# A causal depthwise convolution split over engines: a fourth 128-channel tile leaves TensorE for ScalarE products and GpSimd sums

## What is computed

```python
x = x + 0.5 * _swiglu_ffn(_rmsnorm(x, ffn_norm[i, 0]), ...)
h = _rmsnorm(x, mix_norm[i])
# mixer of layer 0
ab = h @ w_in + b_in;  a, b = split(ab);  u = a * sigmoid(b)
u = depthwise_causal_conv(u, dw) + dw_b        # 31 taps for each of 1024 channels
u = silu(layernorm(u, ln_g, ln_b))             # over the 1024 channels
m = u @ w_out + b_out
# mixer of layer 1: causal differential attention, 8 heads
x = x + m
x = x + 0.5 * _swiglu_ffn(_rmsnorm(x, ffn_norm[i, 1]), ...)
```

## Time and profile before

| | us |
|---|---|
| median of 3 runs | 974.65 (973.72 to 975.8) |
| profiled execution, its own time | 976.0 |
| its span in the trace | 974.2 |
| TensorE busy | 965.4 (99%) |
| VectorE busy | 768.0 (79%) |
| ScalarE busy | 480.6 (49%) |
| GpSimd busy | 56.4 (6%) |

### The profile page before, as it was taken

The page is one execution under the profiler, slowest core; times in us unless marked ns, Lnnn a source line. Parts: engine busy times, 40 slices in busy tenths (PEclk is TensorE's granted clock), DMA queues, the critical chain, the costliest instruction groups (busy, mean ns, idle before and its releaser), DMA issues.

```text
span 974.2 us, 12520 instructions
## 1 busy us (share of the span) xinstructions
PE 965.4 (99%) x4539; PEld 798.4 (82%) x4539; DVE 768.0 (79%) x1445; ACT 480.6 (49%) x751; POOL 56.4 (6%) x75
## 2 busy tenths in 40 slices
PE   8999999999999999999999999999999999999998
PEld 6788888888988888888888888888778788888887
DVE  6758787877967988888788878787768889888872
ACT  6635353465235444444544535354777764444431
POOL 0200000010200200000000000000333100000000
PEclk9999999999999999999999999999999999999999
DMA  8974545562853754545455463635423455454521
GB/s 288 344 310 161 227 155 232 203 235 103 254 178 135 238 215 174 210 178 204 185 195 216 150 238 147 241 142 203 173 87 130 174 180 197 185 205 183 198 104 43
DMA packets 29660, 185.62 MB, mean 191 GB/s; under 512 B 3504, under 2 KB 3632, under 8 KB 9392
## 3 DMA queue, kind: packets, MB, share of 16 engines
q1 hardware_dynamic: 25056, 169.88, 45.8%
q0 software_dynamic: 4416, 15.09, 4.9%
q10 hardware_dynamic: 144, 0.07, 0.0%
HBM read 183.98 MB, written 1.05 MB: 190 GB/s over the span
## 4 chain that ended last, share of the span: by engine, by line
PE 95%; DMA 2%; DVE 1%; ACT 1%; issue 0%; POOL 0%; ACTq 0%
PE pg L470 17%; PE pg L474 16%; PE pg L476 16%; PE acc L470 13%; PE acc L476 13%; PE acc L474 13%; PE acc L661 3%; PE pt L559 1%; PE acc L771 1%; DVE w_lo L1263 1%; DMA raw<-in_units 1%; DMA diags<-in_conv_diags 1%; PE pt L790 1%; ACT w_hi L867 0%; PE pt L752 0%; DMA first<-in_first 0%
## 5 line engine op out<-in xcount | busy, mean ns | idle before, releaser
L1263 DVE TENSOR_TENSOR w_lo<-raw,w_hi 128x1024 fp32r<-128x1024 f32 x316 | 370.4, 1222 | 17.2 <-ACT w_hi L867 16.0
L867 ACT CAST w_hi<-raw 128x1024 fp32r<-128x1024 f32 x316 | 313.2, 1047 | 14.6 <-DMA raw<-in_units 14.4
L470 PE MATMUL pg<-w_hi,a_hi 128*128 128x512 f32 x720 | 283.1, 393 | 0.0
L476 PE MATMUL pg<-w_hi,a_lo 128*128 128x512 f32 x720 | 280.7, 390 | 0.0
L474 PE MATMUL pg<-w_lo,a_hi 128*128 128x512 f32 x720 | 280.6, 390 | 0.0
L1385 DVE STREAM_TRANSPOSE mix<-hs 32x128 f32<-32x128 f32 x592 | 179.2, 303 | 8.9
L470 PEld LDWEIGHTS pg<-w_hi,a_hi 128*128 128x128 f32 x720 | 135.3, 188 | 29.3 <-issue 1.4
L476 PEld LDWEIGHTS pg<-w_hi,a_lo 128*128 128x128 f32 x720 | 135.3, 188 | 28.1
L474 PEld LDWEIGHTS pg<-w_lo,a_hi 128*128 128x128 f32 x720 | 135.3, 188 | 26.9
L1377 DVE SCALAR_TENSOR_TENSOR hs<-pg,rstd,hs 128x256 f32<-128x256 f32 x80 | 38.4, 484 | 103.4 <-ACT hs L912 103.4
L912 ACT ACTIVATE hs<-pg,rstd 128x256 f32<-128x256 f32 x80 | 37.9, 475 | 162.5 <-PE pg L476 162.5
(11 more groups left out here) (147 smaller groups left out, 661.7 us busy)
## 6 DMA issues: line engine op xcount, KB each, us to landing
raw<-in_units SPq DMA_DIRECT2D x158, 1024.0 KB, 5.3
diags<-in_conv_diags POOLq DMA_DIRECT2D x20, 512.0 KB, 4.8
raw<-in_units SPq DMA_DIRECT2D x8, 256.0 KB, 6.2
gain<-in_ffn_norm POOLq DMA_DIRECT2D x3, 512.0 KB, 5.2
xs<-in_x SPq DMA_DIRECT2D x4, 256.0 KB, 5.9
gain<-in_mix_norm POOLq DMA_DIRECT2D x2, 512.0 KB, 6.2
xg<-in_conv_b_in POOLq DMA_DIRECT2D x2, 512.0 KB, 4.3
out_y<-xs SPq DMA_DIRECT2D x4, 256.0 KB, 2.0
```

What stands on the lines that cost most here:

```text
L470: mm = pe.matmul(dst[j], stat_hi, m_hi, start=first, stop=False)
L476: mm = pe.matmul(dst[j], stat_lo, m_hi, start=False, stop=last)
L867: nc.scalar.copy(w_hi[n % RING][:, cols], raw[n % RAW][:, cols]).then_inc(hi_done, 1)
L1263: nc.vector.tensor_tensor(w_lo[n % RING][:, cols], raw[n % RAW][:, cols], w_hi[n % RING][:, cols].bitcast(F32), ALU.subtract).then_inc(lo_ ...
```

## The change

Tile 3 (128 channels) leaves TensorE. ScalarE multiplies its shifted rows by the weights, 31 products of 128x256. GpSimd adds them, two products (128x512) at a time, and lastly adds the two halves. So VK is 4, DVE_TILES is 3, GROUPS falls from 10 to 8 and the diagonal halves from 20 to 16. The products lie in the memory of the sigmoid (`pair_sum`) and in one half of the gain buffer. VectorE's sums lie in PSUM from its 16th tap on. Its order changes: more taps before `glu(3)`, tile 2 lags by 7, the addition of `b_out` moves behind the `rest` calls, and two `tick`s are cut into halves that stand elsewhere. SyncE issues diagonal loads 4 to 15, behind its load of unit u+12. TensorE's order of turns changes.

```diff
-VK = 3
+VK = 4
+DVE_TILES = 3
+PAIRS = -(-W // 2)
-EARLY = 4
-TAPS_DONE = [VK * W - EARLY - 2, VK * W - EARLY - 1, VK * W]
+AT_CHUNK = [4, 9, 15]
+LATE = 7
+TAPS_DONE = [DVE_TILES * W - LATE - 2, DVE_TILES * W - LATE - 1, DVE_TILES * W]
+        pair_sum = sil.rearrange("p t n -> p (t n)")
+        def pair_at(p):
+            return gain[:, 1, p % 2 * 2 * T:(p % 2 + 1) * 2 * T] if p else pair_sum
# SyncE
+            def load_diags(h):
+                sp.wait_ge(diag_used, h - DIAG_RING + 1)
+                sp.dma_start(diags[:, h % DIAG_RING, :], conv_diags[h]).then_inc(diag_loaded_again[h % DIAG_RING], 16)
             for n in range(PIECED, UNITS):
                 load(n)
+                if n == UNIT0[CONV] + 12:
+                    for h in range(DIAG_RING, HALVES):
+                        load_diags(h)
# GpSimd
+            def sum_pair(p):
+                n = min(2, W - 2 * p) * T
+                pool.wait_ge(product_done, min(2 * p + 2, W))
+                if p > 1:
+                    pool.wait_ge(pair_summed, p - 1)
+                nc.gpsimd.tensor_tensor(pair_sum[:, 0:n], pair_sum[:, 0:n], pair_at(p)[:, 0:n], ALU.add).then_inc(pair_summed, 1)
                 if kind == "turn" and a == CONV:
-                    for h in range(DIAG_RING, HALVES):
-                        load_diags(h)
+                    for p in range(1, PAIRS):
+                        sum_pair(p)
+                    pool.wait_ge(pair_summed, PAIRS - 1)
+                    nc.gpsimd.tensor_tensor(cv[:, DVE_TILES, :], pair_sum[:, 0:T], pair_sum[:, T:2 * T], ALU.add) \
+                        .then_inc(pair_summed, 1)
+                    pool.wait_ge(pair_summed, PAIRS)
+                    load_gain(a + 2)
# TensorE, order of the turns
-                for g in range(2, 6):
-                    taps(g)
+                taps(2)
+                taps(3)
                 pe.wait_ge(u_placed, KT)
+                taps(4)
+                taps(5)
+                for g in range(3):
+                    turn_group(g)
+                turn_group(3).then_inc(c_turned, 1)
                 taps(6)
-                for g in (2, 3):
-                    turn_group(g)
-                taps(7)
-                turn_group(4)
-                turn_group(5).then_inc(c_turned, 1)
-                taps(8)
-                turn_group(6)
                 turn_tile(0)
                 turn_tile(1).then_inc(c_turned, 1)
-                turn_group(0)
-                turn_group(1)
-                turn_tile(2).then_inc(c_turned, 1)
-                taps(9)
-                turn_group(7)
-                turn_group(8)
-                turn_group(9).then_inc(c_turned, 1)
+                taps(7)
+                turn_tile(2)
+                turn_tile(3).then_inc(c_turned, 1)
+                for g in range(4, 7):
+                    turn_group(g)
+                turn_group(7).then_inc(c_turned, 1)
# ScalarE
+                def products(p0, p1):
+                    if p0 == 0:
+                        act.wait_ge(chunk_out, 2 * (c0 + chunks))
+                    for p in range(p0, p1):
+                        if p >= 3:
+                            act.wait_ge(pair_summed, p - 2)
+                        for j in range(2 * p, min(2 * p + 2, W)):
...
+                            mm.then_inc(product_done, 1)
                 sigmoids(chunks - 1)
+                products(0, 3)
                 take(0)
+                products(3, 4)
                 take(1)
                 place(chunks - 1)
+                products(4, 6)
                 for g in range(2, GROUPS):
                     take(g)
-                    if g in (4, 6):
-                        round_half(u + 2 * chunks + AHEAD, (g - 4) // 2)
+                    products(min(3 * g, PAIRS), min(3 * g + 3, PAIRS))
+                    if g in (5, 6):
+                        round_half(u + 2 * chunks + AHEAD, g - 5)
# VectorE
+                def dve_sum(k, j):
+                    if AT_CHUNK[2] - (LATE if k == 2 else 0) <= j < W - 1:
+                        return pg[:, k // 2, k % 2 * T:(k % 2 + 1) * T]
+                    return cv[:, k, :]
+                def both(j0, j1):
+                    for j in range(j0, j1):
+                        tap(0, j)
+                        tap(1, j)
+                        if j >= LATE:
+                            tap(2, j - LATE)
                 glu(0)
-                dve.wait_ge(b_out_loaded, 16)
-                for t in range(TT):
-                    mm = nc.vector.tensor_tensor(xs[:, t, :], xs[:, t, :], b_out, ALU.add)
-                link(mm)
                 tick(u + 2)
                 tick(u + 3)
+                both(0, AT_CHUNK[0])
                 glu(1)
+                both(AT_CHUNK[0], AT_CHUNK[0] + 3)
                 tick(u + 4)
+                both(AT_CHUNK[0] + 3, AT_CHUNK[1])
                 glu(2)
+                both(AT_CHUNK[1], AT_CHUNK[2])
                 tick(u + 5)
                 glu(3)
+                both(AT_CHUNK[2], W)
+                for j in range(W - LATE, W):
                     tap(2, j)
+                    if j in (W - 5, W - 3):
+                        rest_half(u + 6 + AHEAD, (j - W + 5) // 2)
                 for n, j in enumerate((2, 0, 1, 3)):
                     dve.wait_ge(c_turned, n + 1)
                     mm = stats(j)
-                    if n == 0:
-                        tick(u + 6)
-                    if n == 2:
-                        tick(u + 7)
                 for kt in range(2, KT):
                     rest(kt)
+                    if kt < 4:
+                        rest_half(u + 7 + AHEAD, kt % 2)
+                dve.wait_ge(b_out_loaded, 16)
+                for t in range(TT):
+                    mm = nc.vector.tensor_tensor(xs[:, t, :], xs[:, t, :], b_out, ALU.add)
+                link(mm)
                 for w in range(3):
                     tick(u + 2 * chunks + w)
```

More of the change, by code:

```diff
@@ L270, in trunk @@
         diag_loaded = [sem(f"diag_loaded{i}") for i in range(DIAG_RING)]
+        diag_loaded_again = [sem(f"diag_loaded_again{i}") for i in range(DIAG_RING)]
         diag_used = sem("diag_used")
@@ L279, in trunk @@
         tap_done = sem("tap_done")
+        product_done = sem("product_done")
+        pair_summed = sem("pair_summed")
         c_turned = sem("c_turned")
@@ L391, in load_diags @@
             def load_diags(h):
-                if h >= DIAG_RING:
-                    pool.wait_ge(diag_used, h - DIAG_RING + 1)
-                pool.dma_start(diags[:, h % DIAG_RING, :], conv_diags[h]).then_inc(diag_loaded[h % DIAG_RING], 16)
+                pool.dma_start(diags[:, h, :], conv_diags[h]).then_inc(diag_loaded[h], 16)
+            def sum_pair(p):
[4 more added lines that the diff above has]
+                nc.gpsimd.tensor_tensor(pair_sum[:, 0:n], pair_sum[:, 0:n], pair_at(p)[:, 0:n], ALU.add).then_inc(pair_summed, 1)
             def set_bias(h):
@@ L435, in _ @@
                     pool.dma_start(b_out, conv_b_out[0].partition_broadcast(P)).then_inc(b_out_loaded, 16)
-                if kind == "turn" and a < 4:
+                if kind == "turn" and a < 4 and a != CONV:
                     if a:
@@ L657, in taps @@
                     for h in (2 * g, 2 * g + 1):
-                        pe.wait_ge(diag_loaded[h % DIAG_RING], 16 * (h // DIAG_RING + 1))
+                        if h < DIAG_RING:
+                            pe.wait_ge(diag_loaded[h], 16)
+                        else:
+                            pe.wait_ge(diag_loaded_again[h % DIAG_RING], 16 * (h // DIAG_RING))
                         for i in range(SHIFTS // 2):
@@ L672, in turn_tile @@
                 def turn_tile(k):
-                    pe.wait_ge(tap_done, TAPS_DONE[k])
+                    if k < DVE_TILES:
+                        pe.wait_ge(tap_done, TAPS_DONE[k | 1 if k < 2 else k])
+                    else:
+                        pe.wait_ge(pair_summed, PAIRS)
                     for i in range(2):
@@ L1016, in take @@
                     nc.scalar.activation(cv2[:, g, :], sums(g), ACT.Identity, bias=group_b[:, g:g + 1]).then_inc(cv_taken, 1)
+                def products(p0, p1):
[5 more added lines that the diff above has]
+                        for j in range(2 * p, min(2 * p + 2, W)):
+                            dst, src = pair_at(p)[:, j % 2 * T:(j % 2 + 1) * T], up[:, DVE_TILES, j:j + T]
+                            weight = chan[:, DVE_TILES, j:j + 1]
+                            if j == 0:
+                                mm = nc.scalar.activation(dst, src, ACT.Identity, bias=chan[:, DVE_TILES, W:W + 1], scale=weight)
+                            else:
+                                mm = nc.scalar.activation(dst, src, ACT.Copy, scale=weight)
+                            mm.then_inc(product_done, 1)
                 act.wait_ge(table_loaded, 16)
@@ L1453, in tap @@
                         dve.wait_ge(tap_done, tapped[k])
```

(21 more changed lines are left out.)

## The result

| | before | after |
|---|---|---|
| median of the runs | 974.18 us (4 runs) | 965.18 us (964.27 to 966.07, 4 runs) |
| profiled execution, own time | 976.0 | 964.57 |
| its span | 974.2 | 962.8 |
| TensorE busy | 965.4 | 954.9 |
| GpSimd busy | 56.4 | 68.9 |

The ratio of the runs is 0.9906, 95% interval 0.9892 to 0.9919: 0.9% faster, or 9.2 us. I had forecast 967.5 in a range of 965.7 to 971.0. So the direction holds, and TensorE's own work came off as forecast.

What follows compares the result with a forecast made beforehand. TensorE, busy 99% of the span, was taken as the bound: 7.2 us saved there less 0.3 for the next stage made 6.9, rounded to 7.1, so 974.65 - 7.1 = 967.5 us, range 965.7 to 971.0.

Steps and rivals of the forecast that it cites:

- TensorE's own work: Convolution stage: two tap groups (7.14 us) and five transposes (0.58) saved, 0.5 charged in the tail; net 7.2 at the statistics.
- Loads: Diagonal loads in the convolution stage: TensorE's stall waiting for them left at 1.0 us, bounds 0 and 2.5.
- Into the next stage: The moved `b_out` addition delays ticks ahead of the next stage's `update`; 0.3 us charged, bounds 0 and 0.7.
- The sum: Whole kernel: 7.2 - 0.3 = 6.9 us faster, rounded to 7.1; 974.65 - 7.1 = 967.5 against the median.
- VectorE: Convolution taps: VectorE done at 268.1, 4 us before TensorE asks for tile 2; PSUM sums cost 0 extra a tap.
- Rival 2: VectorE is the bound, by PSUM taps 0.13 dearer or rest halves held up by GpSimd: 2 to 3 us lost, 970.0; chance 0.06.
- GpSimd: Tile 3's additions: chain from about 252, 12 at 1.35 us plus 1.3, ending at 269.5, before tile 3 is wanted at 272.6.
- The slack of 3: GpSimd's chain of additions was to end 3 us before TensorE wants tile 3.
- rival 1: GpSimd's additions are the bound, at 1.6 to 2.2 us each; at 1.9, 3.6 us lost, 971.1; chance 0.12.
- One of my signs: Ahead of the takes in the convolution stage, ScalarE would wait for TensorE and not for GpSimd.
- Rival 4: Slower than before: GpSimd additions of 2.33 us, from a dear second input or contention; 1.5 us lost, 976.2; chance 0.04.
- Rival 3: Diagonals late behind unit u+12 in SyncE's queue, a stall of 2.5 us or more: 969.0 or above; chance 0.06.

## Why the forecast was right in kind and too small

- **TensorE's own work** (forecast 7.2 net at the statistics). The stage without load stalls is 44.31 before and 36.94 after: 7.37. Right, with its parts: two groups of 3.57 and five transposes make the forecast 7.72 at the end of the taps exactly, and 0.4 is given back in the tail (`stats(3)` starts 1.35 after the taps instead of 0.98), where I had charged 0.5.
- **Loads: the step that failed.** I wrote "I leave the stall at 1.0". Even in the profile that I read, loads cost 1.4 (45.70 - 44.31) and not 1.0. I had counted the one gap (it stands ahead of the fourth group, `taps(3)`, and not of the third, as I wrote), and neither the slow groups behind it nor the eighth, 3.97 in place of 3.74:

```profile
267.88 3.97 PE L661 MATMUL acc<-mix,diags 128*128 128x128 f32 x32
```

  On average over four profiles they cost 1.1 before. In all eight profiles of changed versions they cost 0.1 at most. That is 1.1 too little gain. What removes it is shown in part only: not SyncE's issue (it stalls in the kernel before too), and not u+12's place (no stall with either order). With all groups and full loads, the longest landing was 6.2, 6.3 and 6.2 us in the three profiles with a gap of over half a microsecond, 5.4 in the one without, and 4.7 to 5.7 in the changed versions. Why sixteen loads at this rate have a late one so often, and twelve never had, I can't say.
- **Into the next stage** (0.3 charged): 687.46 and 687.49, so nothing. `update` did start 0.6 later, counted from the first projection matmul (0.7 forecast), and the next stage's first turn by TensorE at 21.51 in both: it was hidden wholly.
- **The sum**: 7.37 + 1.1 = 8.5 against my 7.1, to which I had rounded up 6.9. The runs say 9.2 (7.9 to 10.5) and, measured again beside the kernel before, 8.5 (7.1 to 9.8). So of the 2.3 between 967.5 and 965.18, 1.4 is the sum's, and most of that the loads'. Another 0.5 is the number that I subtracted from: with a fourth run the median of before is 974.18 and not 974.65. The last half microsecond is inside the interval. The range's lower end, 965.7, already had no stall and no charges; it is this median that carried the time below it.
- **The profiled execution**: forecast 968.9, measured 964.57. Of the 4.3, 2.8 are no success of the change: the profile that I read was the latest of all at the first tap group, 241.04, and the one after the earliest, 238.28. That did no harm to the forecast of the median, since the sum was made of differences.
- **VectorE**: last tap forecast 27.1 after the first tap group, measured 27.8, the difference being the rest halves held up by GpSimd. A PSUM tap costs nothing extra, 481 ns as in SBUF, as L1377 had told; the 62 cycles more that follow from the Trainium skill's figures (VectorE: DVE Perf Modes, the TRN2 errata) do not show. Rival 2 falls: the rest halves were held up, by 1.2 in all, and inside VectorE's slack.
- **GpSimd**: chain start forecast 11.0 after the first group, measured 10.98. An addition 1.35 forecast, 1.27 measured, 1.42 from start to start. That it came so near was partly luck: its fixed part is 0.19 and not 0.37, and a column costs 2.1 ns and not 1.9. The end forecast at 28.5, measured 29.7. What I had left out are the additions held up by the two rest halves: the twelve take 17.92, and 16.35 where they aren't disturbed. I had put the rest halves "inside the slack" and taken nothing off it. Tile 3 was wanted at 30.3 and not 31.6, as the stall was gone. The slack of 3 was 0.5, and rival 1 stood much nearer than its price suggested. One of my signs was also wrong: ScalarE did wait for GpSimd, eleven times, but TensorE never had to wait for a `take` because of it. From the view of waits, total, times and longest:

```profile
ACT gain L1070 <- POOL hs L424: 5.0, 11, 1.0
```

  Rival 4's reading, a second input as dear as the first, is out.
- **Rival 3** (diagonals late behind u+12) falls, and the reverse order is what costs.

## What to carry to other kernels

When an engine that is the bound loses work, list who ends next and how long after; here, with VectorE's old order, about three quarters of the gain would not have come. When GpSimd does arithmetic beside VectorE, keep one of VectorE's two inputs in PSUM. A stall that a single profile shows for a transfer is one draw of several: profile the unchanged kernel more than once, measure its whole cost against a version with cheap transfers, and only then decide what the changed kernel keeps of it.

## What was not expected of the hardware

- Where both read SBUF, GpSimd's 1.27 us additions stayed at 1.27 while VectorE's 0.48 taps went to 1.16 on average. Beside single rest halves of 1.22, both were held: additions up to 2.07, rest halves up to 2.21.
- An idle TensorE cost more than its wait: after the 10 us with sums in SBUF its next 32 tap instructions took 5.06 at a granted clock of 1.2 GHz, against 3.74 at 2.4.
- A half-MB load issued by SyncE landed after 4.3 us (kernel before) and 4.5 (changed) in the median, against 4.8 when issued by GpSimd, and the longest was 6.3 against 6.2: hardly a difference.
